# A hybrid SSD and mixture-of-experts step: gates at eviction, four-piece updates, shared scale and shift, folded sums, idle products at the layer boundaries

## The reference, cut to what matters

```python
def run_group(x, c, ssm0, conv0, W):
    for l in range(DEPTH):                       # DEPTH = 2
        mod = jax.nn.silu(c) @ W['w_mod'][l] + W['b_mod'][l]
        sh1, sc1, g1, sh2, sc2, g2 = [t[:, None, :] for t in jnp.split(mod, 6, axis=-1)]
        h = rmsnorm(x, W['mix_pre_g'][l]) * (1 + sc1) + sh1
        z, xbc, dt_raw, u, v, ga, gb = split_cols(h @ W['w_in'][l], IN_SIZES)
        ya, hs, cs = ssd_branch(z, xbc, dt_raw, conv0[l], ssm0[l], ...)
        yb, vr = chunk_mlp_branch(jax.nn.gelu(u), jax.nn.gelu(v), ...)   # layernorm of v
        merged = sigmoid(ga) * (ya @ W['w_ssd_out'][l]) + sigmoid(gb) * (yb @ W['w_cmlp_out'][l])
        x = x + g1 * rmsnorm(merged @ W['w_o'][l], W['mix_post_g'][l])
        h = rmsnorm(x, W['ffn_pre_g'][l]) * (1 + sc2) + sh2
        if l % 2 == 0:
            f = swiglu(h, W['ffn_wg'][0], W['ffn_wu'][0], W['ffn_wd'][0])
        else:
            f = moe_swiglu(h, W['router_w'][0], W['router_b'][0], ...)   # top 2 of 8 experts
        x = x + g2 * rmsnorm(f, W['ffn_post_g'][l])
```

## Time and profile before

| | |
|---|---|
| time, median of 3 runs | 1867.9 us (1865.79 to 1870.8) |
| the profiled execution's own time | 1868.83 us |
| its span in the trace | 1867.1 us |
| mean granted TensorE clock | 0.954 of full speed |
| busy: TensorE, VectorE, ScalarE | 1740.4, 1344.7, 1033.0 us |

### The profile page before, as it was taken

How to read it: one execution, slowest core, us unless ns; L and a number is a source line. 1 busy time by engine, 2 the same in 40 slices (tenths; PEclk the granted TensorE clock), 3 DMA queues, 4 the chain that set the end, 5 groups by cost and what they waited for, 6 DMA issues and landing times.

```text
span 1867.1 us, 33446 instructions
## 1 busy us (share of the span) xinstructions
PE 1740.4 (93%) x13192; PEld 1621.7 (87%) x13192; DVE 1344.7 (72%) x1442; ACT 1033.0 (55%) x1055; POOL 67.9 (4%) x108
## 2 busy tenths in 40 slices
PE   6999998969999789999868999999999999999994
PEld 4899997959989689998767989899998989898993
DVE  3767858553444587866846888888887888788884
ACT  2445654433333346555335777777776767777771
POOL 4001100000000000100001000000000000000000
PEclk8999998979999889999987999999999999999996
DMA  9989632448885345852325999999999999999980
GB/s 277 284 274 320 197 124 91 147 136 280 285 284 172 115 136 182 261 169 91 124 91 170 342 350 346 339 305 354 345 353 297 352 346 351 319 329 353 344 303 24
DMA packets 379498, 465.10 MB, mean 249 GB/s; under 512 B 10403, under 2 KB 351603, under 8 KB 379378
## 3 DMA queue, kind: packets, MB, share of 16 engines
q1 hardware_dynamic: 372370, 441.65, 72.4%
q0 software_dynamic: 6720, 20.86, 3.6%
q10 hardware_dynamic: 304, 1.08, 0.2%
HBM read 452.84 MB, written 10.92 MB: 248 GB/s over the span
## 4 chain that ended last, share of the span: by engine, by line
PE 89%; DVE 7%; ACT 2%; issue 1%; DMA 1%; DVEq 0%; POOL 0%; SPq 0%; ACTq 0%; POOLq 0%
PE psum L404 12%; PE psum L415 11%; PE psum L409 11%; PE psum L1196 9%; PE psum L1201 9%; PE psum L1198 9%; PE psum L1220 4%; PE psum L1224 4%; PE psum L1221 4%; PE psum L748 2%; PE psum L444 2%; PE psum L1155 1%; PE psum L1172 1%; PE psum L1181 1%; PE psum L901 1%
## 5 line engine op out<-in xcount | busy, mean ns | idle before, releaser
L370 DVE TENSOR_TENSOR wlo<-raw,whi 128x2048 fp32r<-128x2048 f32 x219 | 501.7, 2292 | 108.3 <-ACT whi L365 107.4
L365 ACT ACTIVATE whi<-raw 128x2048 fp32r<-128x2048 f32 x219 | 418.5, 1912 | 31.6 <-PE psum L1224 30.1
L348 DVE TENSOR_TENSOR wlo<-raw,whi 128x2048 fp32r<-128x2048 f32 x113 | 258.7, 2290 | 190.2 <-ACT whi L343 190.0
L404 PE MATMUL psum<-xhi,whi 128*128 128x264 f32 x1584 | 237.0, 304 | 42.7 <-ACT xhi L1284 42.7
L404 PEld LDWEIGHTS psum<-xhi,whi 128*128 128x128 f32 x1584 | 214.3, 200 | 64.1 <-issue 51.2
L343 ACT ACTIVATE whi<-raw 128x2048 fp32r<-128x2048 f32 x113 | 216.1, 1913 | 95.6 <-PE psum L415 75.3
L415 PE MATMUL psum<-xhi,wlo 128*128 128x264 f32 x1584 | 212.8, 287 | 0.0
L409 PE MATMUL psum<-xlo,whi 128*128 128x264 f32 x1584 | 212.3, 288 | 0.0
L1196 PE MATMUL psum<-whi,hghi 128*128 128x256 f32 x1408 | 202.2, 286 | 3.3 <-issue 2.4
L409 PEld LDWEIGHTS psum<-xlo,whi 128*128 128x128 f32 x1584 | 203.2, 192 | 0.0
L415 PEld LDWEIGHTS psum<-xhi,wlo 128*128 128x128 f32 x1584 | 199.6, 190 | 0.0
(11 more groups left out here) (359 smaller groups left out, 1888.2 us busy)
## 6 DMA issues: line engine op xcount, KB each, us to landing
raw<-in_exp_wd_dram SPq DMA_DIRECT2D x76, 1024.0 KB, 5.0
raw<-in_exp_wg_dram SPq DMA_DIRECT2D x72, 1024.0 KB, 6.6
raw<-in_exp_wu_dram SPq DMA_DIRECT2D x72, 1024.0 KB, 7.0
raw<-in_w_in_dram SPq DMA_DIRECT2D x52, 1024.0 KB, 5.5
raw<-in_w_mod_dram SPq DMA_DIRECT2D x17, 1024.0 KB, 5.5
hf<-in_exp_wu_dram SPq DMA_DIRECT2D x16, 1024.0 KB, 6.5
hf<-in_exp_wg_dram SPq DMA_DIRECT2D x16, 1024.0 KB, 6.8
hf<-in_exp_wd_dram SPq DMA_DIRECT2D x12, 1024.0 KB, 4.9
```

What stands on the lines that cost most here:

```text
L348: dve.tensor_tensor(wlo[slot], raw[slot], whi[slot].bitcast(F32), ALU.subtract) \
L365: act.activation(whi[j % R3], raw6[slot], ACT.Copy).then_inc(sem["hi_ready"], 1)
L370: dve.tensor_tensor(wlo[j % R3], raw6[slot], whi[j % R3].bitcast(F32), ALU.subtract) \
L404: pe.matmul(out, whi[slot][:, k, j * P:(j + 1) * P], hi(k), start=first and k == 0, stop=False)
```

## The change

It consists of seven edits.

1. In the first chunk of dt, cmlp_out, ssd_out, w_o and gu (the chunks that have to wait for a new x) the pass with the low part of x comes last of the three. In the rest the order stays.
2. At the three boundaries other than the last, TensorE makes 18 products of the identity with itself before the norm of x, and 22 after it (`keep_busy`). Nothing reads their result.
3. x is updated in four pairs of tiles (multiply, add) instead of two halves; ScalarE squares each pair, and TensorE sums all 8 tiles of squares as they come, without VectorE's fold. The final norm stays as it was.
4. The gate is multiplied in when ScalarE evicts w_o and the wd of layer 0 (`scaled_out`: squares, two scaled copies, one copy of the samples), instead of in the update. VectorE no longer adds in the wd of layer 0.
5. ScalarE does scale and shift of two of the four tiles of each half, VectorE the other two (`modulated_hi`). The router waits for the xhi copy rather than for h.
6. For the layernorm of v VectorE adds the upper four tiles of `vb`, and then of its squares, to the lower four; TensorE sums four tiles instead of eight.
7. The last fold of the modulation moves from behind wd to ahead of it, since scaled_out needs the gate. (Two semaphores are dropped besides, and the memset of `facc` is made in layer 1 alone.)

```diff
+            against_hi(whi, first, False, bool(ready))
+            if not ready:
+                against_lo(False)
...
             pe.wait_ge(sem["lo_ready"], n + 1)
...
+            ins = against_hi(wlo, False, last and not ready)
+            if ready:
+                ins = against_lo(last, True)
             ins.then_inc(sem["w_used"], 1)
...
+        BUSY = (18, 22)
...
+            def keep_busy(count):
+
+                for k in range(count):
+                    pe.matmul(ms[:, 1, 0:P], ident[:, :], ident[:, :], start=True, stop=True)
+
             def norm(v):
-                for c in range(2):
-                    if v == 1:
+                if v == 4 * L:
+                    for c in range(2):
+                        pe.wait_ge(sem["sq_folded"], c + 1)
...
+                else:
+                    for c, ks in enumerate(PAIRS):
                         pe.wait_ge(sem["sq_ready"], squares(v) + c + 1)
-                        ins = sum_tiles(sq1, ms[:, 3, 0:T], HT * c, HT * (c + 1))
-                    else:
-                        pe.wait_ge(sem["sq_folded"], folds(v) + c + 1)
-                        ins = sum_tiles(hf, ms[:, 0, 0:T], HT * c, HT * c + HT // 2, last=HT + HT // 2)
+                        ins = sum_tiles(hf, ms[:, 0, 0:T], ks.start, ks.stop)
                 ins.then_inc(sem["ssq_ready"], 1)
...
                 if l:
+                    keep_busy(BUSY[0])
                     norm(4 * l + 1)
+                    keep_busy(BUSY[1])
...
-                        sum_tiles(vb, ms[:, 2, 0:T]).then_inc(sem["v_sum"], 1)
+                        pe.wait_ge(sem["v_half"], 2 * l + 1)
+                        sum_tiles(hf, ms[:, 2, 0:T], 0, HT, 0, HT).then_inc(sem["v_sum"], 1)
...
+                        pe.wait_ge(sem["v_half"], 2 * l + 2)
+                        sum_tiles(hf, ms[:, 2, 0:T], 0, HT, 0, HT).then_inc(sem["v_ssq"], 1)
...
+                keep_busy(BUSY[0])
                 norm(4 * l + 3)
+                keep_busy(BUSY[1])
...
-                        pe.wait_ge(sem["h_ready"], 2 * (2 * l + 2) - 1 + half)
+                        pe.wait_ge(sem["xs_hi"], 2 * (5 * l + 5) - 1 + half)
...
+                    if l == 0:
+                        mod_fold(pe, NM - 1)
...
-                    mod_fold(pe, NM - 1)
...
+                if src is x and v > 1:
+                    for c, ks in enumerate(PAIRS):
+                        act.wait_ge(sem["x_ready"], 4 * (v // 2 - 1) + c + 1)
+                        act.activation(hf[:, ks, :], x[:, ks, :], ACT.Square).then_inc(sem["sq_ready"], 1)
...
+            def modulated_hi(l, k, v, m):
+
+                sh, sc = mod[:, l, 3 * k * KT:(3 * k + 1) * KT, :], mod[:, l, (3 * k + 1) * KT:(3 * k + 2) * KT, :]
+                for c, ks in enumerate(HALVES):
+                    act.wait_ge(sem["samp_scaled"], 2 * m + c + 1)
+                    for t in range(KT)[ks][HT // 2:]:
+                        ins = act.activation(hf[:, t, 0:S], (hf if m else sq1)[:, t, 0:S], ACT.Identity,
+                                             bias=sh[:, t, 0:1], scale=sc[:, t, 0:1])
+                    ins.then_inc(sem["h_act"], 1)
+                    act.wait_ge(sem["h_act"], 2 * m + c + 1)
+                    act.wait_ge(sem["h_ready"], 2 * m + c + 1)
+                    act.activation(xhi[:, ks, :], hf[:, ks, :], ACT.Copy).then_inc(sem["xs_hi"], 1)
...
+            def scaled_out(l, k, ks, banks):
+
+                g = mod[:, l, (3 * k + 2) * KT:(3 * k + 3) * KT, :]
+                dst = (facc if k else zs)
+                act.activation(hf[:, ks, :], banks, ACT.Square).then_inc(sem["sq_ready"], 1)
+                for j, t in enumerate(range(KT)[ks]):
+                    act.activation(dst[:, t, 0:S], banks[:, j, 0:S], ACT.Copy, scale=g[:, t, 0:1])
+                return act.activation(dst[:, ks, S:T], banks[:, :, S:T], ACT.Copy)
...
+                act.wait_ge(sem["mod_ready"], 4 * l + 2)
+                act_phase(act, ("w_o", l), KT // MT, lambda i, c, banks: scaled_out(l, 0, PAIRS[2 * i + c], banks),
+                          end=l == L - 1, peel=KT // MT // 2)
...
+                    if l == 0:
+                        mod_rows(act, NM - 1)
...
                         for c in range(C - (1 if last else 0)):
                             split_hi(act, n1 + c + 1, i, C, e)
-                    if last:
+                    if l == 0:
+                        act.wait_ge(sem["mod_ready"], 4)
+                        q1 = Q0["wd", l]
+                        for c in range(C * (KT // MT // 2)):
+                            split_hi(act, n1 + c + 1, 0)
+                            if c % len(KG) == len(KG) - 1:
+                                act.wait_ge(sem["w_used"], n1 + c + 1)
+                                pair = (q1 + c // len(KG)) % 2
+                                scaled_out(l, 1, PAIRS[c // len(KG)], acc[:, 2 * pair:2 * pair + 2, 0:T]) \
+                                    .then_inc(acc_free[pair], 1)
+                    elif last:
...
                         .then_inc(sem["samp_scaled"], 1)
-                    for t in range(KT)[ks]:
+                    for t in range(KT)[ks][0:HT // 2]:
...
+                g = mod[:, l, (3 * k + 2) * KT:(3 * k + 3) * KT, :]
+                if v < 4 * L:
+                    q = Q0["w_o", l] if v % 4 == 2 else Q0["wd", l]
+                    for c in (2, 3):
+                        dve.wait_ge(acc_free[(q + c) % 2], (q + c) // 2 + 1)
+                    then(dve.tensor_tensor(src[:, :, S:T], src[:, :, S:T], g[:, :, 1:1 + B], ALU.mult))
+                    norm_inv(v)
+                    for ks in PAIRS:
+                        then(dve.tensor_tensor(src[:, ks, :], src[:, ks, :], bc(rs[:, 0, :], 1, [P, MT, T]), ALU.mult))
+                        dve.tensor_tensor(x[:, ks, :], x[:, ks, :], src[:, ks, :], ALU.add).then_inc(sem["x_ready"], 1)
+                    return
...
                     if c == 0:
+                        q = Q0["v", l] + IN_CHUNKS["v"] - 1
+                        dve.wait_ge(acc_free[q % 2], q // 2 + 1)
+                        dve.tensor_tensor(hf[:, 0:HT, :], vb[:, 0:HT, :], vb[:, HT:KT, :], ALU.add).then_inc(sem["v_half"], 1)
...
+                        dve.wait_ge(sem["v_sq"], l + 1)
+                        dve.tensor_tensor(hf[:, 0:HT, :], hf[:, 0:HT, :], hf[:, HT:KT, :], ALU.add).then_inc(sem["v_half"], 1)
...
+                        mod_keep(dve, NM - 1)
```

More of the change, by code:

```diff
@@ L399, in products, with against_hi, against_lo @@
             outs = [acc[:, 2 * pair + j, 0:cols] for j in range(tiles)]
-            for j, out in enumerate(outs):
-                for k in range(nk):
-                    if ready and j == 0 and k % HT == 0:
-                        pe.wait_ge(sem["xs_hi"], 2 * ready - 1 + k // HT)
-                    pe.matmul(out, whi[slot][:, k, j * P:(j + 1) * P], hi(k), start=first and k == 0, stop=False)
-            for j, out in enumerate(outs):
-                for k in range(nk):
-                    if ready and j == 0 and k % HT == 0:
-                        pe.wait_ge(sem["xs_lo"], 2 * ready - 1 + k // HT)
-                    pe.matmul(out, whi[slot][:, k, j * P:(j + 1) * P], lo(k), start=False, stop=False)
+            def against_hi(w, first, last, wait=False):
+                for j, out in enumerate(outs):
+                    for k in range(nk):
+                        if wait and j == 0 and k % HT == 0:
+                            pe.wait_ge(sem["xs_hi"], 2 * ready - 1 + k // HT)
+                        ins = pe.matmul(out, w[slot][:, k, j * P:(j + 1) * P], hi(k), start=first and k == 0,
+                                        stop=last and k == nk - 1)
+                return ins
+            def against_lo(last, wait=False):
+                for j, out in enumerate(outs):
+                    for k in range(nk):
+                        if wait and j == 0 and k % HT == 0:
+                            pe.wait_ge(sem["xs_lo"], 2 * ready - 1 + k // HT)
+                        ins = pe.matmul(out, whi[slot][:, k, j * P:(j + 1) * P], lo(k), start=False,
+                                        stop=last and k == nk - 1)
+                return ins
+            against_hi(whi, first, False, bool(ready))
+            if not ready:
+                against_lo(False)
             if between:
@@ L412, in products @@
             pe.wait_ge(sem["lo_ready"], n + 1)
-            for j, out in enumerate(outs):
-                for k in range(nk):
-                    ins = pe.matmul(out, wlo[slot][:, k, j * P:(j + 1) * P], hi(k), start=False,
-                                    stop=last and k == nk - 1)
+            ins = against_hi(wlo, False, last and not ready)
+            if ready:
+                ins = against_lo(last, True)
             ins.then_inc(sem["w_used"], 1)
@@ L514, in hybrid_ssd_chunkmlp_moe_step @@
         HALVES = (slice(0, HT), slice(HT, KT))
+        PAIRS = [slice(k, k + MT) for k in range(0, KT, MT)]
```

(35 more changed lines are left out.)

53 lines of the change are left out of this document (24 added, 29 removed).

## The result

The changed kernel takes 1850.19 us (median of 7 runs, 1840.18 to 1860.27), the kernel before, timed beside it, 1870.52 us (1865.79 to 1872.42); the ratio is 0.9902, 95% interval [0.988, 0.9924]. The forecast was 1847.3, faster, with a range of 1842 to 1857. The profiled execution took 1855.94 us, its span 1853.9 us.

What follows compares the result with a forecast made beforehand. TensorE, busy 93% of the span, was taken as the bound, its waits mostly at boundary chains over ScalarE and VectorE. Terms of -18.25 us and -2.3 for clock gave -20.6, so 1847.3 us, range 1842 to 1857.

Steps and rivals of the forecast that it cites:

- first norm: At the start, sharing scale and shift makes ScalarE's second high copy end later: +0.5 us.
- fold of v, both layers: VectorE's folds halve TensorE's sums for v: -3.7 us in layer 0, -1.65 in layer 1, together -5.35.
- boundary to gu, second copy: From w_o to gu in layer 0: -3.45 us root to root, -0.8 from sharing, together -4.25.
- fold ahead of wd: At wd's start TensorE first waits for ScalarE's modulation eviction and the last modulation fold: +1.4 us.
- end of layer 0: Boundary wd to dt: root -2.25 us, update -3.45, sharing -0.85, together -6.55.
- router, routing's start: Boundary w_o to router: routing starts 4.0 us earlier, carried through the expert stage because transfers start there: -4.0.
- clock: Idle products hold TensorE's clock at and behind boundaries: 0 to -4.65 us, half taken, -2.3.
- low part last, evictions: Low-part pass last in waiting chunks, and evictions with the gate hidden behind TensorE's chunks: 0 us each.
- Folds late: Rival: VectorE's queue slips, so TensorE waits for folds of v; price 5.35 us, 1852.7; chance 0.14.
- ScalarE as the bound: Rival: a ScalarE tile takes 0.8, not 0.55, second copy 1.0 later at four places; +4.0 us, 1851.3; chance 0.08.
- Gain given back in the expert stage: Rival: transfers ran ahead of the routing, so the last boundary's 4.0 us are lost; 1851.3; chance 0.08.
- Idle products at half clock: Rival: idle products at boundaries do not hold the clock and delay TensorE; 1873.3 to 1882 us; chance 0.13.

Runs made afterwards that it cites:

- e4: Changed kernel without sharing: VectorE again does scale and shift of all eight tiles, ScalarE only the copy; 1853.3 us, ratio 0.9916.
- e10: Changed kernel with idle products in every wait for a new x, last modulation fold inside wd, no sharing at first norm, v not folded; 1846.7 us.
- e2: Changed kernel with no idle products at all; 1854.6 us, ratio 0.9917.
- e12: Changed kernel with the pass of the low part of x second again, as before the change; 1843.0 us, ratio 0.9868.
- e1: Changed kernel run again without any edit; 1851.9 us, ratio 0.9907.
- e3: Changed kernel with the fold of v undone, TensorE summing eight tiles twice in each layer; 1851.6 us, ratio 0.9905.
- e6: Changed kernel with the last modulation fold moved inside the first chunk of wd; 1849.6 us, ratio 0.9886.
- e5: Changed kernel with 44 instead of 22 idle products behind the norm; 1852.1 us, ratio 0.9907.
- e11: Changed kernel with idle products in every wait for a new x and at the start, last fold inside wd, no sharing at first norm; 1840.3 us.
- e8: Changed kernel with idle products also in the first chunk of ssd_out of both layers; 1844.4 us, ratio 0.9861.

## Why the prediction was right, point by point

| term | predicted | measured in the trace after |
|---|---|---|
| first norm | +0.5 | +0.3 (e4 does without it) |
| fold of v, both layers | -5.35 | -5.2 by the rows; 4.7 lost without it in e10 |
| boundary to gu, second copy | -4.25 | -4.25 (21.34 to 17.09) |
| fold ahead of wd | +1.4 | +1.44 at the first product, kept to the end of wd (65.83 behind the copy for 64.39) |
| end of layer 0 | -6.55 | -6.9 (root 2.6 earlier, -3.45, -0.85) |
| router, routing's start | -4.0 | -4.3 (root to root -3.45, routing 14.32 behind the second root for 15.16) |
| clock | -2.3 | about -3 by the traces (e2), most of it inside the boundaries |
| low part last, evictions | 0 | 0 (e12) and no wait for an eviction |

The terms without the clock come to -18.9 where the forecast said -18.25, and each row of the chains is within 0.5 of its term. No run takes back the update in pairs or the gate at eviction (edits 3 and 4), the largest terms; for them the rows stand alone, which repeat within 0.02 in every trace with the changed kernel's idle products (root to root 9.87 to 9.89).

**Where it was off** is the clock. In the profiled execution the span is 13.2 shorter, 6 less than the chains give, because steps of the clock to 0.50 fell in layer 0's gb, for longer than before behind the waits of both ssd_out (10.2 us for 6.8), and at w_o of layer 1; in the median it is 20.3 shorter, by the ratio 18.3. The step of the working that said "I take half" of 4.65 put the gain in the wrong place. Inside the boundaries the idle products held the clock (1.00 for 0.65), and that shortened the sums. Without them root to root is 11.29, 10.15 and 11.30 (e2), so 1.4 of the 3.45 at two boundaries is their doing, though the forecast booked it as a length of the chain "without clock", with a sum of a pair taken from a row at full clock. Behind the boundaries, where the forecast had put the gain, the chunk to gu ran at 0.50 as before in the changed kernel's profile and in e1's, and at 1.00 in those of e3, e6 and e12. That the median lies 3 from the forecast is luck in part: executions of this one program lie 20 apart. The likeliest case's range, 1843 to 1852, is narrower than that, 1840 to 1860; the wider one held for the median.

**The rivals.** Folds late: true of the first sum of layer 1 alone, which the sum had in it. ScalarE as the bound: two tiles take 1.09, the forecast had 1.1; with sharing undone the copy came 0.91 later (e4), not earlier. Gain given back in the expert stage: no, TensorE's products there come 12.7 earlier than before at its start and 13.5 at its end. Idle products at half clock: 0.23 each at 1.00 at the boundaries; and in e5 even twice as many behind the norm left the median where it was. One figure of this rival was off by its own rows: 18 products, full speed for 2.8 us and 0.48 each behind it, take 5.3 and not 5.9, so its 7.9 a boundary should have been 7.3.

The Trainium skill ("TensorE: Matmul & The Clock Gate", section "Part 1: The HAM clock gate") calls the loss to the clock's ramp under 1% of a typical span, and variable from run to run. The variation agrees. In size this case is another one, since the clock steps down 16 and 12 times in the two traces of the changed kernel: executions of one program differ by 20 us of 1850 with their clock, 1.1%. With idle products in more waits the median is 10 lower (e11 against the changed kernel, about 1.3 of it from the two small edits).

## What to carry to other kernels

Cost a boundary as one chain over the engines, from rows of the same size, and each term comes out within about half a microsecond. Note at which clock each row ran: a chain costed from rows at full clock already counts on that clock. Price the clock apart: before tuning a program whose executions spread, look where TensorE waits for some microseconds and at the granted clock of the chunk behind, and try filling these waits, all of their gaps, with products whose result is overwritten. When the spread is the clock's, compare edits at equal clock or hold the clock first; a median of five runs hid a term of 5 us here.

## What the runs showed of the hardware

Products without use made the kernel before 6.1 us faster, ratio 0.997 [0.9958, 0.9981]. In e1 the clock fell to 0.50 in or between the waits ahead of ssd_out (4.7 and 2.4 us) and stayed there for 6.8 and 10.2 us, much of it full work; with idle products in these waits it stayed at 1.00 (e8). In the changed kernel's profile it also fell once while TensorE worked without a gap, on products with 16 of the 128 rows. Where it falls differs between executions of one program, and their times lie 20 us apart along with their mean clock.
